# Differential attention: one reciprocal for both softmax maps of a row, with the first scaling and the lambda product behind it on GpSimd

## What is computed

```python
s1 = einsum(q1b, k1) * scale + bias
s2 = einsum(q2b, k2) * scale + bias
a = softmax(s1) - lam * softmax(s2)
o = einsum(a, v)            # bias: ALiBi slope times distance, or -1e30 where masked
```

## Time and profile before

| what | value |
|---|---|
| median of 3 runs | 2600.49 us (2598.81 to 2601.46) |
| span of the profiled execution | 2600.7 us |
| stretch of the four heads of differential attention | about 432 to 802 us |
| TensorE busy, whole span | 98% |
| VectorE busy, whole span | 62% |
| GpSimd busy, whole span | 13% |

### The profile page before, as it was taken

How to read it: one execution, slowest core, us unless ns; L and a number is a source line. 1 busy time by engine, 2 the same in 40 slices (tenths; PEclk the granted TensorE clock), 3 DMA queues, 4 the chain that set the end, 5 groups by cost and what they waited for, 6 DMA issues and landing times.

```text
span 2600.7 us, 35372 instructions
## 1 busy us (share of the span) xinstructions
PE 2540.5 (98%) x12220; PEld 2114.9 (81%) x12220; DVE 1614.7 (62%) x3499; ACT 1212.5 (47%) x2183; POOL 332.0 (13%) x368
## 2 busy tenths in 40 slices
PE   8999999999999999999999999999999999999997
PEld 7998888777667999977877888888888888888886
DVE  6123306998995776654458677876757465564765
ACT  6112314777764555554544333533335353443554
POOL 1110002222221222210000000000000001111143
PEclk9999999999999999999999999999999999999999
DMA  7334458553332111135677767657655365776787
GB/s 232 122 106 125 126 163 253 143 135 87 93 131 90 36 31 45 41 110 158 194 247 220 221 200 237 218 182 216 190 161 179 110 221 108 171 167 162 203 162 137
DMA packets 329436, 398.59 MB, mean 153 GB/s; under 512 B 21408, under 2 KB 235664, under 8 KB 320944
## 3 DMA queue, kind: packets, MB, share of 16 engines
q1 hardware_dynamic: 311696, 364.41, 44.7%
q0 software_dynamic: 17568, 31.99, 8.4%
HBM read 239.86 MB, written 156.48 MB: 152 GB/s over the span
## 4 chain that ended last, share of the span: by engine, by line
PE 62%; DVE 3%; DMA 1%; ACT 1%; issue 1%; SPq 0%; POOL 0%; DVEq 0%; ACTq 0%; POOLq 0%
PE ff_ps_x L3262 26%; PE ff_ps_m L3262 13%; PE ff_ps_z L3262 6%; PE ml_ps_s L2139 6%; PE ff_ps_m L1695 4%; PE ml_ps_o L2168 4%; PE ml_ps_t L2152 2%; DMA ml_v_raw<-scr_yT 1%; DMA ff_pieces<-scr_acc 0%; PE ff_ps_r L2699 0%; PE mo_ps_t L2716 0%; SPq L2326 0%; DVE ff_pieces L2429 0%; DVE ff_pieces L2620 0%; DVE ff_pieces L2616 0%
## 5 line engine op out<-in xcount | busy, mean ns | idle before, releaser
L3262 PE MATMUL ff_ps_x<-ff_mv_hi_p,ff_st_hi_p 128*128 128x512 f32 x764 | 297.8, 390 | 0.5 <-ACT ff_u L3002 0.5
L3262 PE MATMUL ff_ps_x<-ff_mv_hi_p,ff_st_lo_p 128*128 128x512 f32 x764 | 297.3, 389 | 0.0
L3262 PE MATMUL ff_ps_x<-ff_mv_lo_p,ff_st_hi_p 128*128 128x512 f32 x764 | 297.2, 389 | 0.0
L2139 PE MATMUL ml_ps_s<-wide,ml_qs 128*128 128x416 f32 (+14 forms) x880 | 195.6, 356 | 3.7 <-PEq L137 2.7
L3108 DVE TENSOR_TENSOR ff_st_lo_p<-ff_ps_m,ff_st_hi_p 128x512 fp32r<-128x512 f32 x190 | 130.8, 689 | 103.4 <-ACT ff_st_hi_p L2985 103.4
L2952 POOL DMA_DIRECT2D scr_acc<-ff_pieces x64 | 55.5, 872 | 1015.3 <-DVE ff_pieces L3132 946.9
L3002 ACT ACTIVATE ff_u<-ff_ps_x 128x512 f32<-128x512 f32 x128 | 76.6, 598 | 215.0 <-PE ff_ps_x L3262 215.0
L3262 PEld LDWEIGHTS ff_ps_x<-ff_mv_hi_p,ff_st_hi_p 128*128 128x128 f32 x764 | 143.4, 188 | 32.4 <-issue 2.0
L3262 PEld LDWEIGHTS ff_ps_x<-ff_mv_hi_p,ff_st_lo_p 128*128 128x128 f32 x764 | 143.4, 188 | 29.9
L3262 PEld LDWEIGHTS ff_ps_x<-ff_mv_lo_p,ff_st_hi_p 128*128 128x128 f32 x764 | 143.4, 188 | 29.6
L2139 PEld LDWEIGHTS ml_ps_s<-wide,ml_qs 128*128 128x128 f32 x880 | 152.0, 191 | 16.3 <-issue 2.9
(11 more groups left out here) (318 smaller groups left out, 6349.7 us busy)
## 6 DMA issues: line engine op xcount, KB each, us to landing
st_raw<-in_w_ff SPq DMA_DIRECT2D x64, 512.0 KB, 6.2
scr_hid<-ff_pieces SPq DMA_DIRECT2D x128, 256.0 KB, 2.7
st_raw<-scr_hid SPq DMA_DIRECT2D x64, 512.0 KB, 5.4
ring<-in_w_ff SPq DMA_DIRECT2D x28, 1024.0 KB, 7.7
scr_t<-ring SPq DMA_DIRECT2D x24, 1024.0 KB, 5.8
ring<-scr_t SPq DMA_DIRECT2D x21, 1024.0 KB, 8.1
scr_acc<-ff_pieces POOLq DMA_DIRECT2D x64, 256.0 KB, 4.1
ring<-scr_u SPq DMA_DIRECT2D x13, 1024.0 KB, 8.4
```

The costliest lines, as they stand in the source:

```text
L2139: m = pe.matmul(ps_s[n % NSB][:, 0:w], q, k, start=j == 0, stop=j == len(pairs) - 1)
L3262: m = pe.matmul(bank[:, :], w[kind][:, k], a[kind][:, k], start=start and k == 0 and i == 0, stop=stop and k == KH - 1 and i == 2, skip_gr ...
```

## The change

The step "scale" is replaced by "inverse", put off by 3 chunks behind the last chunk of map **1**. In it VectorE waits for the exponentials of both maps and inverts both sums in one instruction. GpSimd then scales the first map and, behind that, multiplies the second inverse with minus lambda into one of four `ratio` slots. "end" on VectorE waits for both and does only the last multiply-add. The read of a chunk multiplies by minus scale and keeps a minimum, so a map of one chunk (rows 0 to 2) needs no further instruction before the exponential, and the others need a plain minimum over the chunks.

```diff
@@ row_steps
-                        if c == 0:
-                            later.append((SCALE_AFTER, ("scale", 0, i)))
                         if c == COMPS - 1:
+                            later.append((SCALE_AFTER, ("inverse", 0, i)))
                             later.append((END_AFTER, ("end", 0, i)))
...
-        SCALE_AFTER, END_AFTER = 2, 5
+        SCALE_AFTER, END_AFTER = 3, 5
@@ GpSimd
                 hold(pool, inv_ready, NT * h + i + 1)
                 pool.tensor_scalar(row(i, u), row(i, u), inv[:, i % 2, 0:1], 1.0, ALU.mult, ALU.mult).then_inc(first_scaled, 1)
+                if not (isinstance(h, int) and h == 0 and i < RATIOS):
+                    hold(pool, probs_ready, NT * h + i - RATIOS + 1)
+                pool.tensor_scalar(ratio[:, i % RATIOS:i % RATIOS + 1], inv[:, i % 2, 1:2], lam[:, 3:4], 1.0, ALU.mult, ALU.mult).then_inc(ratio_ready, 1)
@@ ScalarE, exp
-                act.wait_ge(max_ready, NT * COMPS * h + COMPS * i + c + 1)
-                act.activation(..., ACT.Exp, bias=nmax[:, i % 2, c:c + 1], scale=scale, ...)
+                if pieces_of(i) > 1:
+                    act.wait_ge(max_ready, MANY * COMPS * h + COMPS * (i - FEW) + c + 1)
+                else:
+                    act.wait_ge(scores_read, NCH * h + first_chunk(i) + c + 1)
+                if not (isinstance(h, int) and h == 0 and i < 2):
+                    act.wait_ge(inv_ready, NT * h + i - 1)
+                act.activation(..., ACT.Exp, bias=nmax[:, i % 2, c:c + 1], scale=-1.0, ...)
@@ VectorE, chunk
-                                         in1=bias[u][:, b0:b0 + w], scale=1.0, scalar=LOWEST,
-                                         op0=ALU.add, op1=ALU.max,
-                                         accum_out=mx[:, i % 2, c, nth:nth + 1]).then_inc(scores_read, 1)
-                if k0 + w == META + P * (i + 1):
+                                         in1=bias[u][:, b0:b0 + w], scale=-scale, scalar=-LOWEST,
+                                         op0=ALU.add, op1=ALU.min,
+                                         accum_out=lowest).then_inc(scores_read, 1)
+                if k0 + w == META + P * (i + 1) and k0 > 0:
                     dve.wait_ge(scores_read, NCH * h + n + 1)
-                    dve.tensor_scalar(nmax_all[:, 0:nth + 1], mx[:, i % 2, c, 0:nth + 1], -scale, None, ALU.mult, ALU.min,
-                                      accum_out=nmax[:, i % 2, c:c + 1]).then_inc(max_ready, 1)
+                    dve.tensor_reduce(out=nmax[:, i % 2, c:c + 1], in_=mx[:, i % 2, c, 0:nth + 1], axis=AX.X, op=ALU.min).then_inc(max_ready, 1)
@@ VectorE, sums and end
-            def invert(h, i, u, **at):
-                dve.wait_ge(exp_ready, NT * COMPS * h + COMPS * i + 1)
-                ... wait first_scaled of row i - 2
-                dve.reciprocal(inv[:, i % 2, 0:1], total[:, i % 2, 0:1]).then_inc(inv_ready, 1)
+            def inverse(h, i, u, **at):
+                dve.wait_ge(exp_ready, NT * COMPS * h + COMPS * (i + 1))
+                ... wait ratio_ready of row i - 2
+                dve.reciprocal(inv[:, i % 2], total[:, i % 2]).then_inc(inv_ready, 1)
             def end(h, i, u, **at):
-                dve.wait_ge(exp_ready, NT * COMPS * h + COMPS * (i + 1))
-                dve.reciprocal(inv[:, i % 2, 1:2], total[:, i % 2, 1:2]).then_inc(inv2_step, 1)
-                dve.wait_ge(inv2_step, n + 1)
-                dve.tensor_scalar(inv2[:, i % 2:i % 2 + 1], inv[:, i % 2, 1:2], lam[:, 3:4], None, ALU.mult).then_inc(inv2_step, 1)
-                dve.wait_ge(inv2_step, n + 2)
+                dve.wait_ge(ratio_ready, NT * h + i + 1)
                 dve.wait_ge(first_scaled, NT * h + i + 1)
```

More of the change, by code:

```diff
@@ L1181, in attention @@
         NTB = 3
+        RATIOS = 4
         pT = mem.sb(f"da_pT", [P, NPT, 512])
@@ L1184, in attention @@
         nmax = mem.sb("da_nmax", [P, 2, COMPS])
[L1185 removed]
         total = mem.sb("da_total", [P, 2, COMPS])
         inv = mem.sb("da_inv", [P, 2, COMPS])
[L1188 removed]
+        ratio = mem.sb("da_ratio", [P, RATIOS])
         lam = mem.sb("da_lam", [P, 4])
@@ L1203, in attention @@
         inv_ready, first_scaled, probs_ready = (mem.sem(f"da_{s}") for s in ("inv_ready", "first_scaled", "probs_ready"))
-        inv2_step = mem.sem("da_inv2_step")
+        ratio_ready = mem.sem("da_ratio_ready")
         pT_ready, pv_done = mem.sem(f"da_pT_ready"), mem.sem("da_pv_done")
@@ L1260, in first_chunk, with pieces_of @@
             return min(n for n, chunk in enumerate(chunks) if chunk[0] == i)
+        def pieces_of(i):
+            return len(row_chunks(i))
+        FEW = sum(pieces_of(i) == 1 for i in range(NT))
+        MANY = NT - FEW
         def cost(step):
@@ L1466, in scaled @@
             def scaled(h, i, u, **at):
+                if isinstance(h, int) and (h, i) == (0, 0):
+                    pool.wait_ge(lam_step, 4)
                 hold(pool, inv_ready, NT * h + i + 1)
                 pool.tensor_scalar(row(i, u), row(i, u), inv[:, i % 2, 0:1], 1.0, ALU.mult, ALU.mult).then_inc(first_scaled, 1)
-            heads(pool, {"scale": scaled})
+                if not (isinstance(h, int) and h == 0 and i < RATIOS):
+                    hold(pool, probs_ready, NT * h + i - RATIOS + 1)
+                pool.tensor_scalar(ratio[:, i % RATIOS:i % RATIOS + 1], inv[:, i % 2, 1:2], lam[:, 3:4], 1.0, ALU.mult, ALU.mult).then_inc(ratio_ready, 1)
+            heads(pool, {"inverse": scaled})
         @stage.scalar
@@ L1475, in exp @@
             def exp(h, i, c, u, **at):
-                act.wait_ge(max_ready, NT * COMPS * h + COMPS * i + c + 1)
-                act.activation(comp_row(i, c, u), comp_row(i, c, u), ACT.Exp, bias=nmax[:, i % 2, c:c + 1], scale=scale,
+                if pieces_of(i) > 1:
[4 more added lines that the diff above has]
+                    act.wait_ge(inv_ready, NT * h + i - 1)
+                act.activation(comp_row(i, c, u), comp_row(i, c, u), ACT.Exp, bias=nmax[:, i % 2, c:c + 1], scale=-1.0,
                                accum_out=total[:, i % 2, c:c + 1]).then_inc(exp_ready, 1)
@@ L1528, in chunk @@
                 b0 = (NT - 1 - i) * P + k0
+                lowest = nmax[:, i % 2, c:c + 1] if pieces_of(i) == 1 else mx[:, i % 2, c, nth:nth + 1]
                 hold(dve, scores_ready, NCH * h + n + 1)
                 dve.tensor_tensor_reduce(out=comp_row(i, c, u)[:, k0:k0 + w], in0=ps_s[n % NSB][:, 0:w],
-                                         in1=bias[u][:, b0:b0 + w], scale=1.0, scalar=LOWEST,
-                                         op0=ALU.add, op1=ALU.max,
-                                         accum_out=mx[:, i % 2, c, nth:nth + 1]).then_inc(scores_read, 1)
-                if k0 + w == META + P * (i + 1):
+                                         in1=bias[u][:, b0:b0 + w], scale=-scale, scalar=-LOWEST,
+                                         op0=ALU.add, op1=ALU.min,
+                                         accum_out=lowest).then_inc(scores_read, 1)
+                if k0 + w == META + P * (i + 1) and k0 > 0:
                     dve.wait_ge(scores_read, NCH * h + n + 1)
-                    dve.tensor_scalar(nmax_all[:, 0:nth + 1], mx[:, i % 2, c, 0:nth + 1], -scale, None, ALU.mult, ALU.min,
-                                      accum_out=nmax[:, i % 2, c:c + 1]).then_inc(max_ready, 1)
+                    dve.tensor_reduce(out=nmax[:, i % 2, c:c + 1], in_=mx[:, i % 2, c, 0:nth + 1], axis=AX.X, op=ALU.min).then_inc(max_ready, 1)
                 if first_head and n == 1:
@@ L1555, in minus_lambda, with end @@
                 dve.wait_ge(lam_step, 4)
-            def invert(h, i, u, **at):
-                dve.wait_ge(exp_ready, NT * COMPS * h + COMPS * i + 1)
-                if not (isinstance(h, int) and h == 0 and i < 2):
-                    dve.wait_ge(first_scaled, NT * h + i - 1)
-                dve.reciprocal(inv[:, i % 2, 0:1], total[:, i % 2, 0:1]).then_inc(inv_ready, 1)
-            def end(h, i, u, **at):
+            def inverse(h, i, u, **at):
                 if isinstance(h, int) and (h, i) == (0, 0):
                     minus_lambda()
-                n = 2 * (NT * h + i)
                 dve.wait_ge(exp_ready, NT * COMPS * h + COMPS * (i + 1))
-                dve.reciprocal(inv[:, i % 2, 1:2], total[:, i % 2, 1:2]).then_inc(inv2_step, 1)
-                dve.wait_ge(inv2_step, n + 1)
-                dve.tensor_scalar(inv2[:, i % 2:i % 2 + 1], inv[:, i % 2, 1:2], lam[:, 3:4], None, ALU.mult).then_inc(inv2_step, 1)
-                dve.wait_ge(inv2_step, n + 2)
+                if not (isinstance(h, int) and h == 0 and i < 2):
+                    dve.wait_ge(ratio_ready, NT * h + i - 1)
+                dve.reciprocal(inv[:, i % 2], total[:, i % 2]).then_inc(inv_ready, 1)
+            def end(h, i, u, **at):
+                dve.wait_ge(ratio_ready, NT * h + i + 1)
                 dve.wait_ge(first_scaled, NT * h + i + 1)
```

(4 more changed lines are left out.)

## The result

The changed kernel takes 2656.83 us (median of 4 runs, 2654.06 to 2658.72) against 2600.89 before: 56 us more, a ratio of 1.0215 with a 95% interval of 1.0203 to 1.0227. The forecast was 2653. The profiled spans are 2655.6 and 2600.7 us.

What follows compares the result with a forecast made beforehand. VectorE was taken to set the pace: pauses for GpSimd less savings gave +15.9 us a head, +63.6 for four, less 10.9 of vanishing waits, so 2600.5 + 52.7 = 2653 us. Range 2636 to 2678, or 2628 to 2678 with rival 2.

Steps and rivals of the forecast that it cites:

- The bound: In the changed stage VectorE sets the pace; TensorE needs at most 79 us a head of the 85 taken.
- The round trip: Row end, VectorE to GpSimd and back: 0.62 us plus the scaling's length, replacing 0.44; VectorE's wait grows to 85 to 95.
- 0 and 1: Rows already waiting for GpSimd: reciprocal to multiply-add grows from 0.82 to 1.00 us, +0.36 a head for both.
- 2 to 9 and 15: Rows with inverse and multiply-add as neighbours: the whole round trip is paid, +11.4 us a head before savings.
- 10 to 14: Rows with one or two chunks between: +4.6 for 10 to 13, +0.85 for 14, +1.3 for exponentials, before savings.
- waits that vanish: VectorE's waits for TensorE (8.4 us) and the first exponential (2.5) go as those engines catch up: -10.9 over four heads.
- rival 2: Pauses hide where TensorE is late, rows 15 and 0 to 8; only rows 9 to 14 pay: 2629 us, chance 0.08.
- The exponentials of rows 10 to 14: The inverse comes after three chunks, when the second map's exponential may not be done: +1.3 us a head.
- Savings: VectorE's shorter scale step (0.08 a row), rows 0 to 2's maxima and the reduce (0.04 a map): -2.6 us a head.
- a sign against itself: TensorE's clock digits falling within the heads would make the prediction wrong, as in rival 3.
- Rivals 1 and 4: 1: TensorE is the bound, 2576 us, chance 0.04. 4: reads or reduces make savings and pauses cancel, same time, chance 0.02.
- rival 3: TensorE's clock falls in the pauses of every row, half the time: +80 us more, 2733, chance 0.04 for the large form.

Runs made afterwards that it cites:

- four-chunk run: The changed kernel with a row's last multiply-add put 4 chunks behind its inverse: 2620.61 us, ratio 1.0069.
- run with one column: The changed kernel with GpSimd's first scaling cut to one column, all steps and waits kept: 2604.72 us, ratio 1.0019.
- two-chunk run: The changed kernel with a row's last multiply-add put 2 chunks behind its inverse: 2626.27 us, ratio 1.0097.
- the run above: The kernel before with its multiply-adds put as late as with 4 chunks between inverse and multiply-add: 2648.66 us, ratio 1.0190.

## Why the prediction was right

**The bound.** That VectorE sets the pace although TensorE is busy 98% was read from the waits, and the runs bear it out on the losing side: outside rows 6 to 8 each row of the changed kernel paid its pause nearly in full. It is less true on the winning side. There TensorE and ScalarE stop rows 5 to 8 at almost the same time whatever VectorE saves. And TensorE's room is smaller than the 79 us a head of the prediction. That took 24 us of waits of the weight loads off the window, but the matmuls were idle for only 11.4 of its 340 us, so more than half of those waits lay beside matmuls that still ran. The waits of the matmuls themselves for VectorE are short (before, 432 to 772 us):

```profile
PE da_ps_s L1609 <- DVE da_mx L1531: 6.1, 10, 1.1
...
PE da_ps_t L1642 <- DVE da_rows L1576: 3.8, 3, 1.3
```

By the busy time of the matmuls, 328.58 us, TensorE's need is an estimated 82 us a head. The sum did not hang on this, since both lie well below 98; the theory of the four-chunk run, with its 79, did.

**The round trip.** Its length was right to 0.01 us in row 9, with errors that cancel (product 0.28 for 0.19, but begun 0.03 before the scaling's recorded end; answer 0.03 for 0.10). The sum of waits over all 64 rows, 85.6 us, lies at the lower end of the 85 to 95 named. That the scaling's length is what is paid is shown by the run with one column, and that the order makes the pause by the two-chunk run.

**The terms of a head**, third head, forecast net of savings against the change of the time from one multiply-add to the next:

| rows | forecast | measured |
|---|---|---|
| 0 and 1 | +0.4 | +0.1 |
| 2 to 9 and 15 | +9.6 | +6.5 |
| 10 to 14 | +5.9 | +5.9 |
| waits that vanish | -2.7 | in the rows above |
| sum | +13.2 | +12.5 |

The mechanism was right and the sizes nearly so. Rows 6 to 8 are where the pauses went into waits for TensorE and ScalarE that were there before: they cost 0.14, 0.09 and -0.17 instead of 1.05 to 1.26 each. That is 3.4 us, more than the 2.7 taken for the whole head; rival 2 was right there, and only there. The exponentials of rows 10 to 14 cost 0.88 us in the third head (0.26 and 0.49 of it in rows 12 and 14) instead of 1.3.

The first head is the check on this. It has no older head's groups to turn and multiply, and before the change its rows 6 to 8 took 15.05 us against 18.03 in the third. There the pause had no wait to hide in, and the three rows paid 0.89, 0.76 and 1.98 us (0.54 of the last is a wait for a chunk, at 470.60, just after the clock had fallen). So the total is closer than its parts: the last three heads came out 0.2 to 0.7 us below the forecast's 13.2 and the first 2.6 above, which the forecast did not set apart. That these partly cancel is luck.

**Savings.** The reduce was taken to save 0.04 a map; it saves nothing (0.24 from read to next chunk, before and after), 4 us less in the sum. Of the 10.9 us of waits taken as gone, 4.4 stayed as waits for chunks. VectorE's busy time on the page of the profile fell by 22.9 us, not 40. The durations of its groups on this stage's tiles add up to 38 less, but the page counts overlapping instructions once. The prediction's sentence that the trace does not agree on the first reciprocal goes too far: the section it cites from the Trainium skill (VectorE: DVE Perf Modes, "The DRAIN you can't avoid") itself says that a next instruction that is not held starts earlier, and a start 0.08 us on does not speak against that.

**The clock** fell at the head borders, as allowed for there, and also three times among the rows of the first two heads, which the prediction had named as a sign against itself. It is a small one: VectorE's waits for chunks, which a slow TensorE would make, are 4.4 us in all, and the third head, with 12.5 us, has no fall among its rows. The last stretch behind the final multiply-add cost 1.3 us.

Rivals 1 and 4 did not happen, and of rival 3 only this small form did. What the forecast did not foresee is what the pause hid: with the pause covered, VectorE waits for TensorE instead. Of the 2621 us the clock in row 12 makes some 4; which part of the rest belongs to late turns, to the borders and to TensorE's own load was not separated. Moving the turns only moved the wait.

## What to carry to other kernels

Before an operation is moved to a helper engine, write down what the leading engine has left to do between handing over and needing the answer; if an order is made by counts with a latest point, that point decides, and here it left nothing in 11 of 16 rows. A handed-over scaling costs its whole length there, and one reciprocal less does not pay for it. Covering such a pause by doing the last step later may only hand it on: here 55 us less of it gave 31 us of time with two chunks of cover, and 75 us less gave 36 with four. Look at what the next engine in order waits for before counting on it.

## What the hardware showed beyond that

- A VectorE multiply-add with two SBUF inputs became longer where GpSimd's scaling ran beside it. 128x1808 took 2919 ns in the run above against 2101 in the kernel before; the overlap was 1.03 us, the excess 0.82. For 128x1552 the excess was 0.67 us at an overlap of 0.88, for 128x144 it was 0.10 at 0.31, and for 128x2064 nothing at 0.21, while 128x1936 without overlap kept 2234. So in this run the multiply-add lost the overlap less about 0.21 us each time, as if it stood still for the rest. GpSimd's scaling kept its 1.88 us. The cause was not isolated; in the kernels before and after the multiply-adds have the same mean (1369 and 1368 ns), so it plays no part in the result.
- A second per-partition factor on GpSimd's scaling is not free: 1270 ns on average instead of 1189, about 0.08 each. ScalarE's 128x512 copy of the output takes 684 ns with a per-partition factor instead of 593.
- A GpSimd tensor_scalar of 128x1 with two per-partition factors lasts 0.27 us, and VectorE starts 0.03 us behind its end (the changed kernel, row 9: 0.28 and 0.03).
